# One inference step of a streaming encoder layer: attention's key blocks in two halves, and two moved steps in the projections

## The chip, the cores and the metric

The kernel runs on one core of one Trainium2 chip. The time is the device time of one execution in microseconds (us). The core's engines run programs of their own and meet through semaphores: TensorE (PE, with its weight loads shown as PEld), VectorE (DVE), ScalarE (ACT), GpSimd (POOL) and SyncE (SP, which issues most of the transfers).

## The reference, cut to what matters

One layer is applied to a prompt of 1024 tokens and to a sample of 8 x 16 tokens. What matters here is stick-breaking attention and the expert layer (PEER) behind it:

```
def sb_attend(q, k, v, q_pos, k_pos):
    z = einsum('bqhd,bkhd->bhqk', q, k) / sqrt(HEAD_DIM)
    mask = k_pos[None, :] < q_pos[:, None]
    log_rest = where(mask, log_sigmoid(-z), 0.0)
    suffix = cumsum(log_rest, axis=3, reverse=True) - log_rest
    a = where(mask, exp(log_sigmoid(z) + suffix), 0.0)
    return einsum('bhqk,bkhd->bqhd', a, v)

# the layer, for the prompt and for the sample
xn = rmsnorm(x);  qa, ka, va, qb, kb, vb, ga, gb = split(xn @ w_in)
x = x + (sigmoid(ga) * (sb_attend(qa, ka, va) @ w_oa) + sigmoid(gb) * (sliding(qb, kb, vb) @ w_ob)) @ w_o
x = x + peer(rmsnorm(x))   # 8 heads x top 16 of 128*128 experts: sum of gelu(u[e] . x) * g * v[e]
return rmsnorm(x)
```

## The kernel before, in words

The kernel is five functions in a row, each with a program for every engine: the sample's part (`sample`, `route_sample`, span time 0 to about 335 us), the prompt's projections (`project`, to 764), the sliding window (`window`, to 865), the routing stage (`decide`, to 1735) and the dense expert layer (`dense`, to the end at 3537.6). The diff touches two of them.

**`project`** multiplies the prompt with `w_in`, in 17 blocks of 256 columns (`NBLK`). A weight block is loaded by SP (`refill`, 1 MB), ScalarE rounds it into a high part (`cast`, L1106), VectorE subtracts that from the weights to have the low part (`split`, L994), and TensorE makes three products of high and low parts (L1144). Buffers for parts are three deep (`WB`); TensorE waits for `w_split`, the count of the low parts made, ahead of each block. ScalarE also moves every sum from PSUM (L1101); it casts block b + 3 when it has done so for block b. SP loads block b + 2 when low part b is made.

Beside that work, VectorE and GpSimd do the sample's experts. GpSimd fetches rows of `peer_uv` by number, one for each token at a time, into a ring of 8 buffers, and VectorE's `fetch` takes them in turn: fetches 0 to 127 are multiplied with the tokens and summed (L1074) into the hidden values `h_sb`, ScalarE applies Gelu to all of them at once (L1131, behind weight block `GELU_BLOCK`), and from fetch 128 on VectorE adds the weighted rows (L1079). `weigh` (L1056 to L1060) makes the experts' weights. The order of `split` and `fetch` on VectorE is written out by hand, 15 (`BETWEEN`) fetches to a split.

**`decide`** goes over 8 query tiles t of 128 tokens, and for each over the key blocks n = 0 to t: 36 pairs. A pair's scores for 8 heads are 128 keys x 1024 (heads x queries), in two PSUM banks of 512 columns each. By engine:

- TensorE: `scores` (L2112) writes them, two blocks ahead of use.
- ScalarE's `front` makes log(1 + exp(-|z|)) in three steps (Abs L1985, Exp L1987, Ln L1989).
- VectorE's `logs` adds max(z, 0) (L1755); first it adds the block before to the running sum (`past_logs`, L1747; L1744 at n = 0).
- TensorE's `rests` adds the sums within the block to the scores (`negtri`, L2138, one matmul for each bank; the trace counts each as two) and those of the blocks before (`negone`, L2142).
- ScalarE's `back` (Exp, L1997) makes the weights, and TensorE's `values` (L2152) multiplies them with v.

Between these steps each engine has work of the expert layer's routing of earlier tiles, placed by tables (`WOVEN`, `MADE`): VectorE's searches for the best scores (MAX8 and the like), one-hot rows on VectorE and ScalarE, their products on TensorE (L2102). A tile ends with the output projections and the router's queries (L2195), whose weights come through a ring `c_chunk` that SP loads.

Of the kernel before, what the change touches and what calls it, by code (L numbers as in the profile page):

```python
# [10 lines left out]
ALU = mybir.AluOpType  # L11
ACT = mybir.ActivationFunctionType
# [10 lines left out]
NBLK = IN_COLS // BW  # L23
# [839 lines left out]
def project(nc, a, o, spent, soft, acc, xg, sc, gw, row_v, w_m, x_parts, w_first):  # L863
# [7 lines left out]
    RB = 8  # L871
    ROWS = 84
    LOW = -3e38
    BETWEEN, GELU_BLOCK, WB = 15, 9, 3
    TAKEN = 2 * P - REST
    before = lambda b: PER_T * b if isinstance(b, int) and b <= MIXED else PER_T * MIXED + NG + NP + NP * (b - MIXED - 1)
    flat = lambda x: x.rearrange("p c q -> p (c q)")
    with ExitStack() as ctx:
# [38 lines left out]
        with nc.Block() as block:  # L917
# [70 lines left out]
            def _(dve):  # L988
                nc.vector.memset(top_f[:], 0.0).then_inc(dve_r.sem, 1)

                def split(b):

                    dve.wait_ge(w_high_done, b)
                    nc.vector.tensor_tensor(w_low[b % WB], wbuf[:, b % 2], w_high[b % WB].bitcast(F32), ALU.subtract).then_inc(w_split, 1)  # L994
# [68 lines left out]
                def fetch(first, last):  # L1063

                    for k in range(first, min(last, TAKEN)):
                        r, s = k % RB, k % P
                        if k == P:
                            dve.wait_ge(act_e.sem, act_e.at(0, "gelu"))
                            dve.wait_ge(dve_g.sem, dve_g.at(0, "g"))
                            nc.vector.tensor_tensor(aw[:], h_sb[:], gw[:], ALU.mult).then_inc(dve_g.sem, 1)  # L1070
                            dve.wait_ge(dve_g.sem, dve_g.at(0, "a"))
                        dve.wait_ge(filled[r], 16 * (k // RB + 1))
                        if k < P:
                            nc.vector.scalar_tensor_tensor(ring[:, r], ring[:, r], 1.0, xg[:], ALU.mult, ALU.mult,  # L1074
                                                           accum_out=h_sb[:, s:s + 1]).then_inc(freed, 1)
                        else:
                            if s:
                                dve.wait_ge(summed, s)
                            nc.vector.scalar_tensor_tensor(acc[:], ring[:, r], aw[:, s:s + 1], acc[:], ALU.mult, ALU.add).then_inc(summed, 1)  # L1079
                            dve.wait_ge(summed, s + 1)  # L1080
                            dve.sem_inc(freed, 1)
# [6 lines left out]
                pairs_best()  # L1088
                split(3)
                experts_of()  # L1090
                fetch(0, BETWEEN)
                weigh()
                for b in range(4, NBLK):
                    split(b)
                    fetch(BETWEEN * (b - 3), BETWEEN * (b - 2))

            @block.scalar
            def _(act):
# [284 lines left out]
def decide(nc, a, o, software, acc, aw, row_v, ring, w_o, dense_in, search, ps):  # L1383
# [27 lines left out]
    with ExitStack() as ctx:  # L1411
        sb = lambda n, s, d=F32: ctx.enter_context(nc.sbuf_tensor(n, s, d))
        sem = lambda n: ctx.enter_context(nc.semaphore(n))
# [10 lines left out]
        soft = [sb("c_soft", [P, D])[:], ring[:, 6], ring[:, 7]]  # L1424
# [31 lines left out]
        wide = lambda b: ps[:, b:b + 2, :].rearrange("p b n -> p (b n)")  # L1456
        Z, SUM, TURN = (2, 0, 6), 4, 5
# [10 lines left out]
        G_st, scattered = [sem(f"c_G_st{n}") for n in range(2)], [software[f"c_scattered{q}"] for q in range(FIRST_HOT)]  # L1468
        dve_past = sem("c_dve_past")
        scored, logged, valued = sem("c_scored"), sem("c_logged"), sem("c_valued")  # L1470
        act_f, weighted = Steps(sem("c_act_front"), "abs exp ln", 0), sem("c_weighted")
        softened, past_done = sem("c_softened"), sem("c_past_done")
        pe_m, pe_r = Steps(sem("c_pe_merge"), "mT wo", -1), Steps(sem("c_pe_router"), "xT sc0 sc1 sc2 sc3", -1)
        act_m, act_r = Steps(sem("c_act_merge"), "oaT mT sq ln rms", -1), Steps(sem("c_act_router"), "xT q0 q1 q2 q3 sc0 sc1 sc2 sc3", -1)
# [9 lines left out]
        with nc.Block() as block:  # L1484
# [216 lines left out]
            def _(dve):  # L1701
# [47 lines left out]
                def logs(t, n):  # L1749

                    p = pair(t, n)
                    if n:
                        past_logs(t, n - 1)
                    dve.wait_ge(act_f.sem, act_f.at(p, "ln"))
                    nc.vector.scalar_tensor_tensor(soft[p % 3], wide(Z[n % 3]), 0.0, soft[p % 3], ALU.max, ALU.add).then_inc(softened, 1)  # L1755

                def best16(j, n, src, vals, idx, names, beside=lambda: None):

# [181 lines left out]
            def _(act):  # L1940
# [38 lines left out]
                def front(t, n):  # L1979

                    p = pair(t, n)
                    act.wait_ge(scored, p + 1)
                    if p >= 3:
                        act.wait_ge(valued, p - 2)
                    nc.scalar.activation(soft[p % 3], wide(Z[n % 3]), ACT.Abs).then_inc(act_f.sem, 1)  # L1985
                    act.wait_ge(act_f.sem, act_f.at(p, "abs"))
                    nc.scalar.activation(soft[p % 3], soft[p % 3], ACT.Exp, scale=-1.0).then_inc(act_f.sem, 1)  # L1987
                    act.wait_ge(act_f.sem, act_f.at(p, "exp"))
                    nc.scalar.activation(soft[p % 3], soft[p % 3], ACT.Ln, bias=1.0).then_inc(act_f.sem, 1)  # L1989

                def back(t, n):

# [94 lines left out]
            def _(pe):  # L2087
# [45 lines left out]
                def rests(t, n):  # L2133

                    p, z = pair(t, n), Z[n % 3]
                    pe.wait_ge(softened, p + 1)
                    for par in range(2):
                        last = nc.tensor.matmul(ps[:, z + par, :], negtri[:], soft[p % 3][:, 512 * par:512 * par + 512], start=False, stop=(n == 0), skip_group_check=True)  # L2138
                    if n:
                        pe.wait_ge(past_done, carried(t, n - 1))  # L2140
                        for par in range(2):
                            last = nc.tensor.matmul(ps[:, z + par, :], negone[:], past[:, 512 * par:512 * par + 512], start=False, stop=True, skip_group_check=True)  # L2142
                    last.then_inc(logged, 1)
# [680 lines left out]
```

## Time and profile before

| what | value |
|---|---|
| median of 3 runs (lowest, highest) | 3539.45 us (3533.47, 3540.75) |
| the profiled execution: its time, its span | 3539.31 us, 3537.6 us |
| TensorE busy, share of the span | 3300.8 us, 93% |
| VectorE busy | 2640.3 us, 75% |
| ScalarE busy | 800.3 us, 23% |
| GpSimd busy | 1494.4 us, 42% |

The time is the span and 1.7 us that lie around it. A busy share is an average over all five stages; which engine waits for which is read stage by stage. PEclk and "granted clock" are TensorE's clock as a share of full speed.

### The profile page before, as it was taken

How to read it: one execution, taken by the hardware profiler on the slowest of the kernel's cores; microseconds unless marked ns; L12 is line 12 of the kernel's file. 1: busy time of each engine (PE TensorE's matmuls, PEld its weight loads, DVE VectorE, ACT ScalarE, POOL GpSimd, SP SyncE). 2: the span in 40 equal slices, each digit the busy share in tenths (PEclk: the TensorE clock that was granted, in tenths of full speed). 3: DMA queues.
4: the chain of work that ended last, by engine and by line, in shares of the span. 5: the costliest groups of instructions: out<-in, count | busy, mean ns of one | idle time of the engine just before them, and what ended most of it. 6: DMA issues, size and time to landing. Idle time of an engine off the chain costs nothing.

```text
span 3537.6 us, 43678 instructions
## 1 busy us (share of the span) xinstructions
PE 3300.8 (93%) x14507; PEld 1960.5 (55%) x14516; DVE 2640.3 (75%) x5015; ACT 800.3 (23%) x1589; POOL 1494.4 (42%) x1116
## 2 busy tenths in 40 slices
PE   9769999986888899999899999999999999999997
PEld 7436789984465667677544444444444444444443
DVE  2555888845468767775699998888888777888888
ACT  3542112215122337675100001000010000100001
POOL 0000388710223778886234443444443433434342
PEclk9989999988999999999899999999999999999998
DMA  8988699956887679889899999999999999999997
GB/s 351 414 340 302 225 406 401 403 180 214 335 303 262 176 193 200 209 165 202 324 416 395 416 382 417 411 404 405 417 389 415 375 391 401 383 406 399 397 416 285
DMA packets 465464, 1196.04 MB, mean 338 GB/s; under 512 B 195672, under 2 KB 257800, under 8 KB 386568
## 3 DMA queue, kind: packets, MB, share of 16 engines
q0 software_dynamic: 149776, 679.68, 50.2%
q1 hardware_dynamic: 183472, 495.29, 37.0%
q10 hardware_dynamic: 132048, 19.01, 3.6%
q8 instruction: 85, 1.39, 0.2%
q14 instruction: 83, 0.68, 0.1%
HBM read 1124.51 MB, written 70.39 MB: 338 GB/s over the span
## 4 chain that ended last, share of the span: by engine, by line
PE 33%; DVE 11%; DMA 3%; issue 3%; POOL 0%; DVEq 0%; ACT 0%; POOLq 0%
PE k_ps L2689 17%; PE k_ps L2675 16%; DVE k_yacc L2439 5%; DVE d_ring L2425 4%; DMA d_ring<-peer_uv,d_idx 3%; DVE k_acc L2439 0%; DMA out_y<-k_acc 0%; DVE d_a L2447 0%; DVE d_qacc L2457 0%; POOL d_ring L2387 0%; DVE e_topi L2477 0%; DVE d_aw L2434 0%; DVE e_top L2472 0%; DVE e_sc L2474 0%; DVE e_ci L2477 0%
## 5 line engine op out<-in xcount | busy, mean ns | idle before, releaser
L2387 POOL DMA_INDIRECT d_ring<-peer_uv,d_idx x512 | 691.1, 1350 | 1004.8 <-DVEq L2441 900.3
L2675 PE MATMUL k_ps<-k_xd,k_ring 128*128 128x512 f32 x2016 | 889.4, 594 | 7.8 <-DMA k_ring<-u_blocks 5.2
L2675 PEld LDWEIGHTS k_ps<-k_xd,k_ring 128*128 128x128 f32 x2016 | 384.2, 191 | 493.1 <-issue 486.3
L2425 DVE SCALAR_TENSOR_TENSOR d_ring<-d_ring,k_xn 128x1024 f32<-128x1024 f32 x512 | 607.5, 1221 | 53.8 <-DMA d_ring<-peer_uv,d_idx 31.4
L1687 POOL DMA_INDIRECT G<-c_cellg,c_cell x256 | 434.3, 1696 | 114.7 <-issue 88.7
L2689 PE MATMUL k_ps<-k_ring,d_a 128*128 128x512 f32 x1024 | 453.0, 595 | 10.8 <-DVE d_a L2447 10.0
L2689 PE MATMUL k_ps<-d_v,d_a 128*128 128x512 f32 x1024 | 451.6, 594 | 2.4 <-DVE d_qacc L2457 2.2
L2439 DVE SCALAR_TENSOR_TENSOR k_acc<-d_ring,d_aw,k_acc 128x1024 f32<-128x1024 f32 x256 | 328.9, 1285 | 45.8 <-DVE k_acc L2439 29.7
L2439 DVE SCALAR_TENSOR_TENSOR k_yacc<-d_ring,d_aw,k_yacc 128x1024 f32<-128x1024 f32 x256 | 328.9, 1285 | 37.0 <-DVE k_yacc L2439 25.4
L2689 PEld LDWEIGHTS k_ps<-k_ring,d_a 128*128 128x128 f32 x1024 | 195.1, 191 | 259.1 <-issue 257.0
L2634 ACT ACTIVATE d_a<-k_ps 128x512 f32<-128x512 f32 x128 | 76.3, 597 | 1140.5 <-PE k_ps L2675 1108.9
L2689 PEld LDWEIGHTS k_ps<-d_v,d_a 128*128 128x128 f32 x1024 | 194.8, 191 | 249.6 <-issue 245.5
L2195 PE MATMUL k_ps<-c_mT,c_chunk 128*128 128x128 f32 x2048 | 248.1, 281 | 18.9 <-DMA c_chunk<-wq 17.8
L2195 PEld LDWEIGHTS k_ps<-c_mT,c_chunk 128*128 128x128 f32 x2048 | 242.4, 198 | 24.7 <-DMA c_chunk<-wq 19.3
L984 POOL DMA_INDIRECT k_merge<-peer_uv,a_rowu x128 | 165.3, 1291 | 180.3 <-DVE k_rowv L1052 140.7
L1074 DVE SCALAR_TENSOR_TENSOR k_merge<-k_merge,k_xg 128x1024 f32<-128x1024 f32 x128 | 153.6, 1225 | 43.6 <-DMA k_merge<-peer_uv,a_rowu 32.6
L1144 PE MATMUL a_ps<-a_w_high,k_x_part 128*128 128x256 f32 x896 | 169.1, 289 | 5.5 <-issue 4.9
L1653 POOL DMA_INDIRECT k_ring<-peer_uv,k_rowv x56 | 66.7, 1190 | 213.8 <-DVE k_acc L1857 95.7
L2630 ACT ACTIVATE d_ge<-d_h (+1 forms) x256 | 49.0, 200 | 475.4 <-DVE d_ring L2425 475.3
L1144 PEld LDWEIGHTS a_ps<-a_w_high,k_x_part 128*128 128x128 f32 x896 | 144.4, 197 | 8.1 <-issue 7.6
L2447 DVE TENSOR_TENSOR d_a<-d_a,d_gb 128x512 f32<-128x512 f32 x128 | 88.2, 690 | 69.1 <-issue 35.6
L1144 PE MATMUL a_ps<-a_w_low,k_x_part 128*128 128x256 f32 x448 | 129.7, 290 | 2.4 <-issue 2.2
(423 smaller groups left out, 4265.5 us busy)
## 6 DMA issues: line engine op xcount, KB each, us to landing
c_chunk<-wq SPq DMA_DIRECT2D x128, 512.0 KB
k_ring<-u_blocks SPq DMA_DIRECT2D x128, 512.0 KB, 21.1
s_kc<-sb_kT SPq DMA_DIRECT2D x32, 1024.0 KB, 13.7
s_vc<-sb_v SPq DMA_DIRECT2D x32, 1024.0 KB, 11.2
c_chunk<-w_m SPq DMA_DIRECT2D x64, 512.0 KB
k_ring<-v_blocks SPq DMA_DIRECT2D x64, 512.0 KB, 9.5
d_gb<-G SPq DMA_DIRECT2D x32, 1024.0 KB
d_v<-v_blocks SPq DMA_DIRECT2D x64, 512.0 KB
```

The costliest lines, as they stand in the source:

```text
L984: pool.indirect_dma_start(out=ring[:, k % RB], out_offset=None, in_=rows, in_offset=bass.IndirectOffsetOnAxis(ap=source[:, k % P:k % P + 1 ...
L1074: nc.vector.scalar_tensor_tensor(ring[:, r], ring[:, r], 1.0, xg[:], ALU.mult, ALU.mult, accum_out=h_sb[:, s:s + 1]).then_inc(freed, 1)
L1144: last = nc.tensor.matmul(out, lhsT(left, k), rhs(right, k), start=(k == 0 and n == 0), stop=(k == KC - 1 and n == 2))
L1687: pool.indirect_dma_start(out=grid, out_offset=bass.IndirectOffsetOnAxis(ap=cell[q][:, s:s + 1], axis=0), in_=cell_g[q][:, s:s + 1], in_of ...
L2195: last = nc.tensor.matmul(ps[:, QUERY[w // 4], (w % 4) * P:(w % 4 + 1) * P], wq[:, c * P:(c + 1) * P], xT[:, c], start=(c == 0), stop=(c = ...
L2387: pool.indirect_dma_start(out=ring[:, b], out_offset=None, in_=a["peer_uv"], in_offset=bass.IndirectOffsetOnAxis(ap=idx8[par][:, b:b + 1], ...
L2425: last = nc.vector.scalar_tensor_tensor(ring[:, b, 0:D], ring[:, b, 0:D], 1.0, xn[T % 2][:], ALU.mult, ALU.mult, accum_out=h[:, bass.ds(co ...
L2439: nc.vector.scalar_tensor_tensor(acc[T % 2][:], ring[:, b, D:], aw[:, bass.ds(col + n, 1)], acc[T % 2][:], ALU.mult, ALU.add).then_inc(sum ...
L2447: nc.vector.tensor_tensor(A[u][j][:], A[u][j][:], gb[u][:, j], ALU.mult).then_inc(gated, 1)
L2634: nc.scalar.activation(A[x // GB][x % GB][:], ps[:, HB + x % 2, :], ACT.Gelu).then_inc(h_gelu, 1)
L2675: last = nc.tensor.matmul(ps[:, HB + x % 2, :], ub[j][:, k], xd[:, k].rearrange("p t q -> p (t q)"), start=(k == 0), stop=(k == KC - 1))
L2689: last = nc.tensor.matmul(ps[:, to, :], A[u][j][:, q * P:(q + 1) * P], vb[u][j][:, half * 512:half * 512 + 512], start=(opens and j == 0), ...
```

## The change

In `project`, `GELU_BLOCK` goes from 9 to 10, so ScalarE's program has the Gelu one weight block later; and each `split` from 4 on stands one step of 15 fetches earlier in VectorE's program. In `decide`, `front`, `logs` and `rests` treat the two banks of a pair one after the other: ScalarE makes Abs, Exp and Ln for the first 512 columns and then for the others, VectorE adds max(z, 0) to each half when its Ln is there, and TensorE waits for each half ahead of its `negtri` products. `past_logs`, `negone`, `back` and `values` stay whole.

```diff
-    BETWEEN, GELU_BLOCK, WB = 15, 9, 3
+    BETWEEN, GELU_BLOCK, WB = 15, 10, 3
...
                 experts_of()
+                split(4)
                 fetch(0, BETWEEN)
                 weigh()
-                for b in range(4, NBLK):
-                    split(b)
-                    fetch(BETWEEN * (b - 3), BETWEEN * (b - 2))
+                for b in range(5, NBLK + 1):
+                    if b < NBLK:
+                        split(b)
+                    fetch(BETWEEN * (b - 4), BETWEEN * (b - 3))
...
-                    dve.wait_ge(act_f.sem, act_f.at(p, "ln"))
-                    nc.vector.scalar_tensor_tensor(soft[p % 3], wide(Z[n % 3]), 0.0, soft[p % 3], ALU.max, ALU.add).then_inc(softened, 1)
+                    for par in range(2):
+                        half = soft[p % 3][:, 512 * par:512 * par + 512]
+                        dve.wait_ge(act_f.sem, act_f.at(p, f"ln{par}"))
+                        nc.vector.scalar_tensor_tensor(half, ps[:, Z[n % 3] + par, :], 0.0, half, ALU.max, ALU.add).then_inc(softened, 1)
...
-                    nc.scalar.activation(soft[p % 3], wide(Z[n % 3]), ACT.Abs).then_inc(act_f.sem, 1)
-                    act.wait_ge(act_f.sem, act_f.at(p, "abs"))
-                    nc.scalar.activation(soft[p % 3], soft[p % 3], ACT.Exp, scale=-1.0).then_inc(act_f.sem, 1)
-                    act.wait_ge(act_f.sem, act_f.at(p, "exp"))
-                    nc.scalar.activation(soft[p % 3], soft[p % 3], ACT.Ln, bias=1.0).then_inc(act_f.sem, 1)
+                    for par in range(2):
+                        half = soft[p % 3][:, 512 * par:512 * par + 512]
+                        nc.scalar.activation(half, ps[:, Z[n % 3] + par, :], ACT.Abs).then_inc(act_f.sem, 1)
+                        act.wait_ge(act_f.sem, act_f.at(p, f"abs{par}"))
+                        nc.scalar.activation(half, half, ACT.Exp, scale=-1.0).then_inc(act_f.sem, 1)
+                        act.wait_ge(act_f.sem, act_f.at(p, f"exp{par}"))
+                        nc.scalar.activation(half, half, ACT.Ln, bias=1.0).then_inc(act_f.sem, 1)
...
-                    pe.wait_ge(softened, p + 1)
                     for par in range(2):
+                        pe.wait_ge(softened, 2 * p + par + 1)
                         last = nc.tensor.matmul(ps[:, z + par, :], negtri[:], soft[p % 3][:, 512 * par:512 * par + 512], start=False, stop=(n == 0), skip_group_check=True)
```

VectorE's program in `project` around the first fetches, before and then in the difference (L1050 and L1052 make the row numbers for the fetches, L1074 is a fetched row's product, L994 a low part):

```order
206 L1049 TENSOR_SCALAR a_h<-a_cand 128x128
207 L1050 CAST a_rowu<-a_h 128x128
208 L1052 TENSOR_SCALAR k_rowv<-a_rowu 128x128
209 L1074 SCALAR_TENSOR_TENSOR k_merge,a_h<-k_merge,k_xg 128x1024 x15
210 L1056 TENSOR_REDUCE a_gsum<-k_aw 128x8
211 L1058 RECIPROCAL a_gsum<-a_gsum 128x8
212 L1060 TENSOR_TENSOR k_aw<-k_aw,a_gsum 128x128
213 L994 TENSOR_TENSOR a_w_low<-k_merge,a_w_high 128x2048
```

```order
 L1050 CAST a_rowu<-a_h 128x128
 L1052 TENSOR_SCALAR k_rowv<-a_rowu 128x128
+L994 TENSOR_TENSOR a_w_low<-k_merge,a_w_high 128x2048
 L1074 SCALAR_TENSOR_TENSOR k_merge,a_h<-k_merge,k_xg 128x1024 x15
 L1056 TENSOR_REDUCE a_gsum<-k_aw 128x8
 L1058 RECIPROCAL a_gsum<-a_gsum 128x8
 L1060 TENSOR_TENSOR k_aw<-k_aw,a_gsum 128x128
-L994 TENSOR_TENSOR a_w_low<-k_merge,a_w_high 128x2048
-L1074 SCALAR_TENSOR_TENSOR k_merge,a_h<-k_merge,k_xg 128x1024 x15
 L994 TENSOR_TENSOR a_w_low<-k_merge,a_w_high 128x2048
```

Low part 4 now stands ahead of the first 15 fetches, and all later ones follow one group of fetches sooner.

ScalarE's program in `project` around the Gelu (L1131; L1133 in the changed kernel), before and then after (L1101 and L1103 are evacuations of sums, L1106 and L1108 casts, ACT_TABLE_LOAD loads a function table):

```order
253 L1101 ACT_TABLE_LOAD
254 L1101 ACTIVATE a_stage<-a_ps 128x256 x8
255 L1106 ACTIVATE k_w_first<-k_merge 128x2048
256 L1131 ACT_TABLE_LOAD
257 L1131 ACTIVATE a_h<-a_h 128x128
258 L1101 ACT_TABLE_LOAD
259 L1101 ACTIVATE a_stage<-a_ps 128x256 x8
```

```order
254 L1103 ACTIVATE a_stage<-a_ps 128x256 x8
255 L1108 ACTIVATE k_w_first<-k_merge 128x2048
256 L1103 ACTIVATE a_stage<-a_ps 128x256 x8
257 L1108 ACTIVATE a_w_high<-k_merge 128x2048
258 L1133 ACT_TABLE_LOAD
259 L1133 ACTIVATE a_h<-a_h 128x128
260 L1103 ACT_TABLE_LOAD
261 L1103 ACTIVATE a_stage<-a_ps 128x256 x8
```

Eight evacuations and a cast now stand ahead of the Gelu and its table loads.

ScalarE's program in `decide`, before (one pair's `back`, then the `front` of the next but one) and after (one `front`; L1991, L1993 and L1995 are its lines there):

```order
521 L1997 ACTIVATE c_soft<-k_ps 128x1024
522 L1951 ACTIVATE c_spread<-k_ps 128x4x128
523 L1985 ACTIVATE k_ring<-k_ps 128x1024
524 L1987 ACTIVATE k_ring<-k_ring 128x1024
525 L1989 ACTIVATE k_ring<-k_ring 128x1024
```

```order
567 L1991 ACTIVATE c_soft<-k_ps 128x512
568 L1993 ACTIVATE c_soft<-c_soft 128x512
569 L1995 ACTIVATE c_soft<-c_soft 128x512
570 L1991 ACTIVATE c_soft<-k_ps 128x512
571 L1993 ACTIVATE c_soft<-c_soft 128x512
572 L1995 ACTIVATE c_soft<-c_soft 128x512
```

Three instructions of 1024 columns became six of 512; on VectorE the one instruction of L1755 became two in the same place.

## Rows read from the trace of the kernel before

**Rows 1.** The page's first part: busy us of each engine (share of the span).

```profile
PE 3300.8 (93%) x14507; PEld 1960.5 (55%) x14516; DVE 2640.3 (75%) x5015; ACT 800.3 (23%) x1589; POOL 1494.4 (42%) x1116
```

**Rows 2.** Windows: length, busy us (count) of PE, PEld, DVE, ACT, POOL, clock, DMA share, GB/s.

```profile
480.00:640.00 160.00, 152.29 (x1144) 146.56 (x1145) 131.39 (x188) 32.43 (x58) 129.16 (x99) 0.94 1.02 403
...
865.00:1735.00 870.00, 784.44 (x4901) 561.96 (x4910) 582.87 (x1880) 370.15 (x596) 500.92 (x312) 0.96 0.83 236
```

**Rows 3.** TensorE's timeline, starts of blocks 4 and 6 [idle before, what ended it].

```profile
431.93 0.80 PE L1144 MATMUL a_ps<-k_x_part,a_w_high 128*128 128x512 f32 x1 [2.16 <-DVE a_w_low L994]
...
479.84 2.93 PE L1144 MATMUL a_ps<-k_x_part,k_w_first 128*128 128x512 f32 x6 [2.57 <-issue]
```

**Rows 4.** VectorE's timeline in `project`: the first fetch, low parts 4 and 6.

```profile
403.66 1.23 DVE L1074 SCALAR_TENSOR_TENSOR k_merge<-k_merge,k_xg 128x1024 f32<-128x1024 f32 x1 [4.66 <-DMA k_merge<-peer_uv,a_rowu]
...
429.59 2.29 DVE L994 TENSOR_TENSOR a_w_low<-k_merge,a_w_high 128x2048 fp32r<-128x2048 f32 x1
...
477.50 2.29 DVE L994 TENSOR_TENSOR k_w_first<-k_merge,k_w_first 128x2048 fp32r<-128x2048 f32 x1
```

**Rows 5.** Windows behind the two waits, and one behind the first's slow stretch.

```profile
431.80:435.20 3.40, 3.27 (x8) 2.59 (x9) 3.40 (x6) 0.90 (x2) 2.58 (x2) 0.50 1.05 414
435.30:438.70 3.40, 3.40 (x16) 2.80 (x16) 3.40 (x8) 0.00 (x0) 3.10 (x2) 1.00 1.01 374
...
479.70:483.00 3.30, 3.16 (x8) 2.49 (x9) 3.30 (x6) 0.60 (x1) 2.88 (x2) 0.50 1.04 423
```

**Rows 6.** ScalarE's timeline in `project`: cast 4, the Gelu, the last evacuation.

```profile
384.36 1.91 ACT L1106 ACTIVATE a_w_high<-k_merge 128x2048 fp32r<-128x2048 f32 x1
...
614.70 0.31 ACT L1131 ACTIVATE a_h<-a_h 128x128 f32<-128x128 f32 x1 [9.50 <-issue]
...
763.37 0.38 ACT L1101 ACTIVATE a_stage<-a_ps 128x256 f32<-128x256 f32 x1 [2.49 <-PE a_ps L1144]
```

**Rows 7.** VectorE's timeline: its last fetched row in `project`.

```profile
734.10 1.28 DVE L1079 SCALAR_TENSOR_TENSOR k_acc<-k_merge,k_aw,k_acc 128x1024 f32<-128x1024 f32 x1 [0.21 <-DVE k_acc L1079]
```

**Rows 8.** One line's view, L1755: idle before it (us, times), and who waited for it.

```profile
  ACT k_ring L1989: 23.2, 8
...
  PE k_ps L2138: 45.4, 24
```

**Rows 9.** Groups by line and shape: instructions of 512 columns (the sample stage's).

```profile
L332 DVE TENSOR_TENSOR s_work<-s_ps,s_work 128x512 f32<-128x512 f32 x32 | 22.1, 691 | 1.1
...
L452 ACT ACTIVATE s_work<-s_work 128x512 f32<-128x512 f32 x32 | 20.2, 631 | 0.0
...
L449 ACT ACTIVATE s_work<-s_ps 128x512 f32<-128x512 f32 x32 | 19.1, 596 | 67.0 <-PE s_ps L611 67.0
```

**Rows 10.** Timelines of three engines in `decide`, pair (4, 1).

```profile
1201.67 1.02 ACT L1985 ACTIVATE k_ring<-k_ps 128x1024 f32<-128x1024 f32 x1 [11.63 <-PE k_ps L2112]
...
1203.81 1.06 ACT L1989 ACTIVATE k_ring<-k_ring 128x1024 f32<-128x1024 f32 x1
...
1204.90 1.23 DVE L1755 SCALAR_TENSOR_TENSOR k_ring<-k_ps,k_ring 128x1024 f32<-128x1024 f32 x1 [0.45 <-ACT k_ring L1989]
...
1206.18 1.98 PE L2138 MATMUL k_ps<-k_ring,c_negtri 128*128 128x512 f32 x4 [1.55 <-DVE k_ring L1755]
```

**Rows 11.** Timelines of VectorE and TensorE in `decide`, tile 7, two pairs in a row.

```profile
1576.62 1.21 DVE L1755 SCALAR_TENSOR_TENSOR k_ring<-k_ps,k_ring 128x1024 f32<-128x1024 f32 x1
...
1581.97 1.20 DVE L1747 TENSOR_TENSOR c_past<-c_past,k_ring 128x1024 f32<-128x1024 f32 x1
1583.24 1.22 DVE L1755 SCALAR_TENSOR_TENSOR c_soft<-k_ps,c_soft 128x1024 f32<-128x1024 f32 x1
...
1577.89 1.99 PE L2138 MATMUL k_ps<-k_ring,c_negtri 128*128 128x512 f32 x4 [0.85 <-DVE k_ring L1755]
```

**Rows 12.** One line's view, L2195: TensorE's idle before the router's queries (us, times).

```profile
  DMA c_chunk<-wq: 37.1, 16
```

**Rows 13.** One line's view, L1997: ScalarE's idle before `back` (us, times).

```profile
  DVE c_past L1747: 30.3, 18
```

More of the change, by code:

```diff
@@ L1470, in decide @@
         scored, logged, valued = sem("c_scored"), sem("c_logged"), sem("c_valued")
-        act_f, weighted = Steps(sem("c_act_front"), "abs exp ln", 0), sem("c_weighted")
+        act_f, weighted = Steps(sem("c_act_front"), "abs0 exp0 ln0 abs1 exp1 ln1", 0), sem("c_weighted")
         softened, past_done = sem("c_softened"), sem("c_past_done")
```

## The prediction

> **What bounds the kernel now.** I read the page's totals first: TensorE is busy 93% of the span, VectorE 75%, ScalarE 23% [rows 1]. A kernel like this loses time only where TensorE stands still or runs slowly, so I took the windows of the two stages that the diff touches, then TensorE's timeline at each of its waits there, and then the lines that it waited for. In the projections TensorE has nearly no idle time except at two places: ahead of weight block 4 it sat idle for 2.16 us until VectorE's low part was made, and ahead of block 6 for 2.57 us [rows 3]. The second carries the label "issue", which names no engine, but VectorE's low part 6 runs from 477.50 to 479.79 and TensorE resumes at 479.84 [rows 3, 4]: that is the same wait. Block 5's low part came in time in between. Behind both waits stands a stretch at a granted clock of 0.50, the lower of the clock's two levels (1.2 instead of 2.4 GHz): 8 matmuls in 3.40 us where 16 fit at 1.00 [rows 5].
>
> In the routing stage TensorE is busy 784.44 of 870 us [rows 2], so 86 us are idle. Of these, 45.4 us in 24 pieces are waits of the `negtri` products for VectorE's L1755, the very step that is cut in two [rows 8]; 37.1 us in 16 pieces are waits for the router's weights from DMA [rows 12]. The first number looks like the prize. The question is whether shortening one link of that chain shortens the chain.
>
> **Projections: what the change takes away.** Low part 4 now stands ahead of the first 15 fetches. There VectorE sits idle 4.66 us until the first fetched row lands at 403.66 [rows 4], and the cast it needs was done at 384.36 + 1.91 = 386.27 [rows 6]. The low part takes 2.29 us [rows 4], so it runs from about 399.0 to 401.3 inside idle time, 28 us ahead of TensorE's need (431.93 - 2.16 = 429.77). Each later low part takes the place of the one before it. Blocks 4 and 5 together take 479.84 - 431.93 = 47.9 us, so a block is some 24 us; part 5 is made at about 429.6 to 431.9 and is needed at about 452, part 6 near 453.5 to 455.8 and needed near 472. Both waits go:
>
> - idle time: 2.16 + 2.57 = 4.73 us [rows 3];
> - the slow stretches: a matmul at full clock takes 3.40 / 16 = 0.2125 us; 8 fewer were done in the first, about 7.5 fewer in the second [rows 5]; 15.5 x 0.2125 = 3.3 us.
>
> Together 8.0 us. TensorE's last sum of the stage is moved out at 763.37, with VectorE done at 734.10 + 1.28 = 735.4 [rows 6, 7], so the stage's end follows TensorE and the 8.0 us reach the end of the kernel: the later stages start when this one ends.
>
> **What could take it back there.** A low part made sooner also releases SP's load of the block after next sooner. It is 1 MB, 2.6 us at the 403 GB/s of [rows 2], and falls among the first fetched rows; they may come 2.6 us later on VectorE, whose slack at the stage's end is 28 us, 20 once TensorE ends 8 sooner. The casts may now be what some low parts wait for, on VectorE, with `fetch` queued behind; I bound this by a few us, against the same slack, since TensorE needs the part a block later.
>
> **The later Gelu.** Gelu waited 9.50 us on ScalarE for VectorE's fetches and ran at 614.70 [rows 6]; eight evacuations were queued behind it, but TensorE's eight banks covered them, and it shows no gap there: no gain on TensorE. Afterwards ScalarE comes to it one block (24 us) later: 24 - 9.5 = 14.5 us, less up to 8 because TensorE is sooner. VectorE has then 6 to 15 us of waiting ahead of fetch 128, and GpSimd's ring stands still behind it. With 735.4 + 15 = 750 against TensorE's new end at about 755, this costs nothing; if the cover were gone, every us past 755 would count in full.
>
> **Attention in halves, on ScalarE.** One pair's front takes 3.20 us now (1201.67 to 1203.81 + 1.06) [rows 10]. No row shows it in halves of this stage; the nearest are the sample's 512-column steps, 0.596 out of PSUM and 0.631 in SBUF [rows 9]. So a half takes 0.60 + 2 x 0.63 and 0.06 between: 1.92 us; both take 3.84 us if nothing overlaps. The first half is ready 1.28 us sooner, the second 0.64 us later than before.
>
> **On VectorE and TensorE.** L1755 takes 1.23 us, and 0.05 later TensorE starts [rows 10]. A 512-column step with two sources takes 0.691 [rows 9]; two take 1.38, at most 0.16 more than one whole.
>
> Two kinds of pairs follow. Where VectorE waits for ScalarE, as in (4, 1) with 0.45 us [rows 10], the second half's product could start at 3.20 + 0.03 + 1.23 + 0.05 + 0.91 = 5.42 after the front's start (0.91 being the first product's share of the 1.98); it will start at 3.84 + 0.03 + 0.69 + 0.05 = 4.61. Gain 0.8 us, inside the 1.55 us of idle time ahead of it. Where VectorE itself is the pace, as in tile 7 (1583.24 follows 1581.97 + 1.20 with no wait, 6.6 us after the last L1755 [rows 11]), TensorE may start after 0.69 instead of 1.22: gain 0.53 us of its 0.85.
>
> But VectorE gets no faster. Its next L1755 stands behind the same searches and running sums, and those have no wait for TensorE to lose. TensorE therefore arrives early and waits longer at the next pair: the gain is had about once a tile, at the last pair, not 24 times. Against it stand up to 0.16 us more VectorE work in each pair. Tiles 4 to 7 have 26 pairs: four gains of 0.53 to 0.8 are 2.1 to 3.2 us, 26 x 0.16 are up to 4.2. The net lies between -3.2 and +2.1; I take 0. Tiles 0 to 3 end in waits for the router's weights from DMA [rows 12], which swallow a us either way. TensorE's 36 added waits are met while the first half's product runs; by the 0.05 us of the row they cost 1.8 at most, and I take nothing.
>
> **Sum.** The profiled execution took 3539.31 us, 0.14 below the median of the runs shown. 3539.31 - 8.0 + 0 = 3531.3, so 3531.
>
> **Rivals.**
>
> *The gains add up.* If TensorE, not VectorE, were the pace of the tiles, each of the 24 waits would lose 0.53: 12.7 us of the 45.4 [rows 8]. For it: the idle time is real and ends at L1755. Against: VectorE runs from one L1755 to the next without a wait in tile 7 [rows 11]. Time 3531.3 - 12.7 = 3518.6.
>
> *Other stalls eat the projections' gain.* From 480 to 640 TensorE loses 160 - 152.29 = 7.7 us idle, at a mean clock of 0.94 (another 9.6), while DMA is at its full share of 1.02 [rows 2]; there "issue" again names no engine. The moved loads and fetches re-phase that stretch. One more such stall, of 2.6 (as [rows 3]) to 8.7 (half of that loss), gives 3534 to 3540. For it: the stretch has such losses already. Against: they may as well shrink.
>
> *Slower: ScalarE becomes the pace.* Its front is 0.64 us longer in each pair. If that lay in the path of tiles 4 to 7, 26 x 0.64 = 16.6 us: 3548. It decides where ScalarE's idle time ahead of `back` is under 0.64 us; now that is 30.3 / 18 = 1.7 us on average, waiting for VectorE's sum [rows 13], and ScalarE is busy only 370 of the stage's 870 us [rows 2]. So this is unlikely, but single pairs will meet it.
>
> The Trainium skill, "VectorE: DVE Perf Modes", section on the TRN2 errata, speaks against the change here: each instruction on VectorE and ScalarE with a source in SBUF pays a fixed latency, so a large tile pays it once and many small ones each time. This trace agrees: 1.06 us for 1024 columns [rows 10] against 0.631 for 512 [rows 9]. By that rule alone, with all of it on the path, the time would be this rival's 3548; by the rows on who waits for whom it is the 3531 of the sum.
>
> *The Gelu comes too late.* If VectorE ended past 755, the stage would end later: 3534 to 3540 for 3 to 9 us past it.
>
> **Chances and range.** Forecast (projections' 8 us, attention about nothing; own range 3526 to 3536) 0.55; gains add up 0.15; other stalls 0.20; ScalarE the pace 0.07; Gelu 0.03. This kernel's measurement tells about 0.2%, 7.1 us, from no change: faster is below 3532.4, slower above 3546.5. Some 0.65 of the forecast's range lies below 3532.4: faster 0.55 x 0.65 + 0.15 = 0.51; same 0.55 x 0.35 + 0.20 + 0.03 = 0.42; slower 0.07. The range goes from the first rival to the second's end, 3519 to 3540, and leaves out the slower rival and the tails, about 0.17.
>
> **What will show it.** Right: no idle time ahead of TensorE's blocks 4 and 6 and no half clock behind them; the last evacuation near 755; VectorE idle ahead of its first L1079 without harm; the sum of TensorE's waits for VectorE's L1755 smaller by much, but moved to the other waits, with the routing stage still about 870 us long. Wrong: a routing stage shorter than 864 us (gains add up) or longer than 876 (ScalarE's idle time ahead of `back` gone, TensorE's `values` waiting for it); or new "issue" gaps between 400 and 640 us.

## The result, and the profile after

The changed kernel takes 3514.8 us (median of 4 runs, 3506.39 to 3518.24), against 3539.74 for the kernel before: a ratio of 0.9929, 95% interval 0.9911 to 0.9947, which is 25 us. Forecast were 3531, with a range of 3519 to 3540. The direction held; the time lies under the range, with three times the gain that the sum had.

The first part of the page, of after, beside [rows 1] (busy us, share of the span):

```profile
PE 3292.3 (94%) x14507; PEld 1953.6 (56%) x14516; DVE 2645.1 (75%) x5051; ACT 819.7 (23%) x1697; POOL 1487.5 (42%) x1116
```

VectorE has 36 and ScalarE 108 instructions more; hardly any busy time has gone. The stages come first, therefore. Each stage's length, from its first instruction to the next stage's first, in the profiled executions:

```
stage          before   after   difference
sample          340.0   342.6     +2.6
projections     428.5   406.8    -21.7
window           94.6   100.0     +5.4
routing         876.5   877.5     +1.0
dense layer    1798.0  1787.0    -11.0
```

The routing stage, where attention was cut in halves, is no shorter. The dense layer, in which no line was changed, is 11 us shorter. The projections give nearly three times the 8.0 us of the sum, in this pair of profiles. (The sample's and the window's differences belong to untouched code; over the runs below these stages lie between 338 and 344, and 94.6 and 100.4, with and without the edits.)

The projections after. VectorE's timeline (low part 4, the last fetched row), ScalarE's (the Gelu, the last evacuation) and TensorE's only idle piece over 0.3 us behind its first matmul there:

```profile
401.58 2.28 DVE L994 TENSOR_TENSOR a_w_low<-k_merge,a_w_high 128x2048 fp32r<-128x2048 f32 x1
...
740.82 1.28 DVE L1079 SCALAR_TENSOR_TENSOR k_acc<-k_merge,k_aw,k_acc 128x1024 f32<-128x1024 f32 x1 [0.26 <-DMA k_merge<-peer_uv,k_rowv]
```

```profile
621.58 0.31 ACT L1133 ACTIVATE a_h<-a_h 128x128 f32<-128x128 f32 x1 [20.02 <-DVE k_merge L1074]
...
739.18 0.38 ACT L1103 ACTIVATE a_stage<-a_ps 128x256 f32<-128x256 f32 x1 [2.49 <-PE a_ps L1146]
```

```profile
623.73 2.50 PE L1146 MATMUL a_ps<-k_w_first,k_x_part 128*128 128x256 f32 x19 [2.67 <-ACT a_stage L1103]
```

Low part 4 runs where it was forecast, and the waits of [rows 3] are gone. But ScalarE now stands 20.02 us at the Gelu for VectorE's fetches (9.50 in [rows 6]), and TensorE has a new wait of 2.67 us, for a sum's bank that ScalarE has not moved out. TensorE's last sum is moved out at 739.56 and VectorE is done at 742.10, but neither ends the stage. SP issues its last two stores of `gates` at 739.59 and 740.81, and the next stage starts at 749.45, when they have landed. SP's wait for them, before and then after:

```profile
SPq L972 <- DMA gates<-a_stage: 3.1, 1, 3.1
```

```profile
SPq L972 <- DMA gates<-a_stage: 7.4, 1, 7.4
```

The line's view of SP's last two loads (`k_merge<-bd`, 1 MB each, issued 15 us ahead of the stores) has 18.4 and 21.4 us from issue to landing, 7.1 and 9.4 before. TensorE's work in the stage, from its first matmul to the end of its last, got 27 us shorter (396.4 for 423.3), the stage only 22.

Windows (columns as in [rows 2]) of the same stretch as there, and of the routing stage and the dense layer by their own bounds, after:

```profile
480.00:640.00 160.00, 157.33 (x1308) 156.41 (x1307) 134.25 (x193) 34.26 (x64) 122.92 (x98) 1.00 1.02 409
...
849.70:1727.20 877.50, 795.87 (x4910) 564.13 (x4918) 586.85 (x1922) 388.67 (x709) 500.84 (x312) 0.95 0.83 235
1727.20:3513.90 1786.70, 1748.89 (x4064) 772.29 (x4064) 1508.66 (x2286) 153.33 (x427) 720.81 (x586) 0.99 0.98 398
```

and the same two stages of before:

```profile
863.10:1739.60 876.50, 788.55 (x4910) 563.48 (x4918) 583.97 (x1885) 373.01 (x600) 500.92 (x312) 0.96 0.83 235
1739.60:3537.60 1798.00, 1754.95 (x4064) 774.11 (x4064) 1507.61 (x2288) 150.61 (x427) 722.89 (x586) 0.99 0.98 396
```

Attention's chain did get shorter link by link. One line's view of who waited for VectorE's step (L1759), after, and of the matmuls' idle time at `values`, before (L2152) and then after (L2158):

```profile
  PE k_ps L2144: 33.6, 25
```

```profile
  DMA c_v<-out_v: 2.8, 2
```

```profile
  DMA c_v<-out_v: 7.9, 2
```

TensorE waits 33.6 us for VectorE's step instead of 45.4 [rows 8], nearly the 12.7 of the first rival. The stage did not follow: the matmuls' wait for `values`' v blocks rose from 2.8 to 7.9 us, and TensorE's busy time rose by 7.3 at a granted clock of 0.95 instead of 0.96. In all, TensorE's idle time there fell by 6.3 us.

### The profile page after: what moved, and what is told of

It is laid out like the page before. It is cut to its first block, busy times and chain, and to the rows that moved or that the text cites. A ratio compares the mean times of both kernels' runs of the same rounds, so it can differ in the third digit from the quotient of the medians.

```text
span 3513.9 us, 43822 instructions
## 1 busy us (share of the span) xinstructions
PE 3292.3 (94%) x14507; PEld 1953.6 (56%) x14516; DVE 2645.1 (75%) x5051; ACT 819.7 (23%) x1697; POOL 1487.5 (42%) x1116
## 4 chain that ended last, share of the span: by engine, by line
PE 36%; DVE 9%; DMA 3%; issue 2%; POOL 0%; DVEq 0%; ACT 0%; POOLq 0%
PE k_ps L2695 18%; PE k_ps L2681 18%; DVE d_ring L2431 3%; DVE k_yacc L2445 3%; DMA d_ring<-peer_uv,d_idx 3%; DVE k_acc L2445 1%; DMA out_y<-k_yacc 0%; DVE d_a L2453 0%; POOL d_ring L2393 0%; DVE d_qacc L2463 0%; DVE e_topi L2483 0%; DVE e_top L2478 0%; DVE d_aw L2440 0%; DVE e_sc L2480 0%; DVE e_ci L2483 0%
## 5 line engine op out<-in xcount | busy, mean ns | idle before, releaser
L1074 DVE SCALAR_TENSOR_TENSOR k_merge<-k_merge,k_xg 128x1024 f32<-128x1024 f32 x128 | 154.3, 1225 | 44.9 <-DMA k_merge<-peer_uv,a_rowu 43.3
L1146 PE MATMUL a_ps<-a_w_high,k_x_part 128*128 128x256 f32 x896 | 161.4, 283 | 0.0
L2453 DVE TENSOR_TENSOR d_a<-d_a,d_gb 128x512 f32<-128x512 f32 x128 | 88.1, 689 | 64.5 <-ACT d_a L2640 25.6
```

What stands on the lines that cost most here:

```text
L1146: last = nc.tensor.matmul(out, lhsT(left, k), rhs(right, k), start=(k == 0 and n == 0), stop=(k == KC - 1 and n == 2))
L2453: nc.vector.tensor_tensor(A[u][j][:], A[u][j][:], gb[u][:, j], ALU.mult).then_inc(gated, 1)
```

## The experiments

Ratios are to the kernel before, measured on the same chip, with 95% intervals. Stage lengths are those of the one profiled execution of each kernel, by the same bounds as above. Edits are shown cut to the lines that matter.

**One part of the change at a time.** Four kernels.

`e1_proj`: the two edits of `project`, with the old `decide`.

> Only the two edits of the projections; attention whole as before. Theory A (the whole gain comes from the projections stage: the two waits for low parts, 8 us, and the instruction gaps of blocks 3, 7 and 8 that went with them, some 15 us; attention gives nothing): about 3516 to 3520, TensorE's work of the stage some 396 us long as in the changed kernel (423 before). Theory B (attention's halves give about half of the gain): 3526 to 3532.

`e2_halves`: the three edits of `decide`, with the old `project`.

> Only attention in halves; the projections as before. Theory A: 3536 to 3541, no change, the routing stage 876 to 878 us. Theory B: 3524 to 3530, with the 11 us of the dense stage shorter as in the changed kernel. The projections of this kernel are a second look at the old order: if the instruction gaps at blocks 3, 7 and 8 come again, they belong to that order; if they lie elsewhere or are missing, they are scatter from run to run.

`e3_splits`: the kernel before with only the low parts sooner.

```diff
-                fetch(0, BETWEEN)
-                weigh()
-                for b in range(4, NBLK):
-                    split(b)
-                    fetch(BETWEEN * (b - 3), BETWEEN * (b - 2))
+                split(4)
+                fetch(0, BETWEEN)
+                weigh()
+                for b in range(5, NBLK + 1):
+                    if b < NBLK:
+                        split(b)
+                    fetch(BETWEEN * (b - 4), BETWEEN * (b - 3))
```

> Only the low parts sooner, Gelu behind block 9 as before. Theory A: the two waits ahead of blocks 4 and 6 are gone, 8 us; ScalarE stands at the Gelu while sums of block 10 pile up, so TensorE may stand up to 10 us there if the fetches have not gained: 3518 to 3532. Rival (the later Gelu is what brings the other part): over 3528.

`e4_gelu`: the kernel before with only this.

```diff
-    BETWEEN, GELU_BLOCK, WB = 15, 9, 3
+    BETWEEN, GELU_BLOCK, WB = 15, 10, 3
```

> Only the Gelu one block later, low parts in the old order. Theory A: no gain by itself, 3536 to 3542, the waits ahead of blocks 4 and 6 as before. Rival (ScalarE's stall at the Gelu was what held TensorE in the projections): 3525 or less.

```
kernel      ratio   95% interval       projections  routing  dense
e1_proj     0.9957  0.9941 to 0.9973      409.1      879.3   1798.1
e2_halves   0.9967  0.9953 to 0.9981      423.3      878.6   1785.7
e3_splits   1.0011  1.0000 to 1.0023      423.3      875.0   1798.2
e4_gelu     0.9994  0.9981 to 1.0006      420.2      878.4   1798.3
```

Theory A was wrong that the whole gain comes from the projections: the halves have 12 us of it. It was right that attention has none: the 12 us are in the dense layer, which is 1798 us long in every kernel of the table with the old `decide`. And neither edit of the projections is worth anything alone: sooner low parts gain nothing, the later Gelu gains nothing, both together gain 15 us.

The rows say why. TensorE's timeline of `e3_splits`, at its only idle piece over 0.3 us behind its first matmul there, and ScalarE's there:

```profile
615.03 0.55 PE L1146 MATMUL a_ps<-a_w_low,k_x_part 128*128 128x256 f32 x1 [21.80 <-ACT a_stage L1103]
```

```profile
612.88 0.31 ACT L1133 ACTIVATE a_h<-a_h 128x128 f32<-128x128 f32 x1 [39.16 <-DVE k_merge L1074]
```

TensorE got past blocks 4 and 6 without waiting, and then stood 21.80 us: ScalarE's program had the Gelu ahead of the evacuations of block 10, the Gelu waits for VectorE's fetch 127, and eight banks of sums were full. What it had won it lost there. The Gelu is a meeting of three engines: VectorE has done 128 fetched rows at about 613 to 622 us in these kernels' profiles, wherever TensorE is, and TensorE cannot get more than eight sums past the block named by `GELU_BLOCK`. The profile of `e2_halves`, with the old `project`, has the same meeting (8.8 to 12.0 us in its profile and those of `e5_act` to `e8_fill128` below, which have the old `project` too):

```profile
619.51 0.55 PE L1144 MATMUL a_ps<-a_w_low,k_x_part 128*128 128x256 f32 x1 [11.63 <-ACT a_stage L1101]
```

In `e4_gelu` the meeting is a block later, but TensorE does not get there sooner, since the low parts are what it waits for, ahead of blocks 4 and 6 as in [rows 3] and then also later. Two rows of its TensorE timeline:

```profile
654.59 0.39 PE L1144 MATMUL a_ps<-a_w_low,k_x_part 128*128 128x256 f32 x1 [2.25 <-DVE a_w_low L994]
680.12 0.39 PE L1144 MATMUL a_ps<-a_w_low,k_x_part 128*128 128x256 f32 x1 [2.24 <-DVE a_w_low L994]
```

So one edit lets TensorE run ahead and the other gives it room to do so. The instruction gaps that the profile of before has in blocks 3, 7 and 8 do not come again in blocks 7 and 8 of `e2_halves` and `e4_gelu`, which have the old order: there they were scatter, and in the execution shown they stood in place of the wait at the Gelu. So that execution is no fair measure of the old order: its projections took 428.5 us, against 419.5 to 423.8 in the five other profiles with the old `project`, and the stage's 21.7 us of gain are some 15 beside those.

**What shortens the dense layer.** Two kernels with one half of the halves each, and two without any.

`e5_act`: the kernel before with ScalarE's `front` in halves, as in the change; VectorE waits for the second Ln and does its step whole.

```diff
-                    dve.wait_ge(act_f.sem, act_f.at(p, "ln"))
+                    dve.wait_ge(act_f.sem, act_f.at(p, "ln1"))
```

> The kernel before, with only ScalarE's front in halves: VectorE's step and TensorE's wait whole again. Theory P (the halves gain nothing in attention; what they gain is 12 us in the untouched dense stage, because VectorE's program is 36 instructions longer ahead of it and its instruction loads fall elsewhere): VectorE's program is as long as before, so the dense stage is 1798 us and the time that of before, or up to 5 us more by the longer front. Theory Q (ScalarE's part is what shifts the dense stage): dense stage 1786, time 12 us under before.

`e6_dve`: the kernel before with VectorE's step and TensorE's wait in halves, both behind the whole Ln; VectorE's edit:

```diff
-                    dve.wait_ge(act_f.sem, act_f.at(p, "ln"))
-                    nc.vector.scalar_tensor_tensor(soft[p % 3], wide(Z[n % 3]), 0.0, soft[p % 3], ALU.max, ALU.add).then_inc(softened, 1)
+                    for par in range(2):
+                        half = soft[p % 3][:, 512 * par:512 * par + 512]
+                        dve.wait_ge(act_f.sem, act_f.at(p, "ln"))
+                        nc.vector.scalar_tensor_tensor(half, ps[:, Z[n % 3] + par, :], 0.0, half, ALU.max, ALU.add).then_inc(softened, 1)
```

> The kernel before, with only VectorE's step and TensorE's wait in halves; ScalarE's front whole. Theory P: 36 more VectorE instructions, the dense stage 1786 us, the routing stage about 877, the time some 10 us under before. Theory Q: dense stage 1798, time as before.

`e7_fill36`: the kernel before, with waits that are already met at the start of VectorE's program in `decide`.

```diff
-                dve.wait_ge(tabs, 64)
+                for _ in range(37):
+                    dve.wait_ge(tabs, 64)
```

> The kernel before with nothing of the change, but 36 waits on VectorE (for a semaphore that has been reached) at the start of the routing stage, where VectorE is idle: only the length of its program changes. Theory P: dense stage 1786 us, time some 10 us under before. Theory R (the halves move the dense stage by what attention hands over: other times, other transfers): dense stage 1798, time as before.

`e8_fill128`: the same with 129 in place of 37.

> As the kernel with 36 such waits, but 128. The trace's instruction loads of VectorE are of 8 KB each; if only the place within such a piece counts, and one instruction is 64 bytes, then 128 instructions shift by a whole piece and theory P gives the dense stage of before again, 1798 us. If the length acts in another way: any value between 1780 and 1805, and not that of the kernel with 36 waits.

Two such waits make one instruction, as the traces' counts show: VectorE's program was 18 and 64 instructions longer, not 36 and 128.

```
kernel       more on VectorE   ratio   95% interval       routing  dense
e5_act             0           1.0013  1.0002 to 1.0024    883.1   1795.2
e6_dve            36           0.9959  0.9945 to 0.9974    879.5   1785.2
e7_fill36         18           0.9974  0.9962 to 0.9987    882.2   1788.1
e8_fill128        64           1.0001  0.9987 to 1.0014    876.0   1797.8
```

Theory P holds against Q and R: a kernel that has nothing of the change but 18 idle waits is 9 us faster than the kernel before, all of it in the dense layer, and with 64 waits the gain is gone. (The expectation on 128 more instructions, by its reckoning a whole 8 KB piece, was not put to the test.) The dense layer of `e5_act` is 2.8 us shorter than that of before; its cause is open.

The rows show what happens. VectorE's timeline of before has this three times (2757, 2869 and 2987 us), here the last, and TensorE's what came of it. The first two held TensorE for 1.1 and 1.7 us, the last for 7.0:

```profile
2987.31 0.69 DVE L2447 TENSOR_TENSOR d_a<-d_a,d_gb 128x512 f32<-128x512 f32 x1 [10.77 <-issue]
```

```profile
2996.67 2.07 PE L2689 MATMUL k_ps<-k_ring,d_a 128*128 128x512 f32 x2 [7.03 <-DVE d_a L2447]
```

VectorE stood 10.77 us for nothing that the profile names. The DMA view of just that idle time (2976.5 to 2987.3) names it, two packets of the queue that loads instructions:

```profile
q0 software_dynamic: 566, 4.08, 91.8%
q1 hardware_dynamic: 95, 0.39, 8.8%
q14 instruction: 2, 0.02, 0.4%
```

The place is a loop's jump back. In the trace the two loads start 5.0 us apart (2980.27 and 2985.30), and VectorE's idle time falls into two pieces of 5.39 and 4.93 us, the first right behind the branch. The changed kernel has five such jumps with one load each, this one the third, and TensorE's idle time is short:

```profile
2526.99 0.69 DVE L2453 TENSOR_TENSOR d_a<-d_a,d_gb 128x512 f32<-128x512 f32 x1 [5.91 <-issue]
```

```profile
2536.34 7.13 PE L2695 MATMUL k_ps<-k_ring,d_a 128*128 128x512 f32 x16 [1.24 <-DVE d_a L2453]
```

In `e8_fill128` the double load is back, at another turn of a loop (VectorE's timeline, then TensorE's):

```profile
2545.99 0.69 DVE L2448 TENSOR_TENSOR d_a<-d_a,d_gb 128x512 f32<-128x512 f32 x1 [10.64 <-issue]
```

```profile
2555.35 5.48 PE L2690 MATMUL k_ps<-k_ring,d_a 128*128 128x512 f32 x6 [6.92 <-DVE d_a L2448]
```

The 7.03 us of TensorE's idle time are followed by a stretch at a lower clock. Windows of before, behind that wait and a little later:

```profile
2996.70:3003.40 6.70, 6.70 (x10) 2.88 (x11) 6.06 (x10) 0.20 (x1) 3.65 (x3) 0.60 0.94 335
3007.00:3013.70 6.70, 6.70 (x17) 2.96 (x16) 6.14 (x10) 0.34 (x1) 2.27 (x2) 1.00 1.02 425
```

Seven matmuls fewer, of 6.70 / 17 = 0.39 us each, are 2.8 us; the clock of 0.60 for 6.70 us says the same, 2.7. So 7.03 + 2.8 = 9.8 us are lost at this jump, most of the 10 to 13 us by which the dense layer is shorter in the kernels without it. The rest, up to 3 us, stays unexplained.

The Trainium skill, "Runtime: NRT & Kernel Launch", section on instruction fetch mechanics, has this rule: a taken branch whose target lies outside the pages that an engine holds forces a load before execution goes on. The runs agree: VectorE stood 5.91 us at a jump with one load here, and 10.77 where two follow one another.

**Whether attention's halves gain anything, and how far the meeting can be moved.** Four kernels on one chip.

`e9_proj_fill`: the edits of `project`, attention whole, and 73 waits as above (36 more VectorE instructions by the count).

> The two edits of the projections, attention whole as before, and 36 more instructions (waits that are met) on VectorE at the start of the routing stage, as many as the halves add there. Theory P+G (the projections gain by the meeting at the Gelu, the rest is the place of VectorE's program in its instruction loads, attention's halves give nothing): dense stage 1786 us, the time that of the whole change, 0.992 to 0.994 of before. Rival (the halves do gain in attention): about 0.9957, as the projections' edits alone, or up to 5 us under it.

`e10_gelu11`: the changed kernel with one number more.

```diff
-    BETWEEN, GELU_BLOCK, WB = 15, 10, 3
+    BETWEEN, GELU_BLOCK, WB = 15, 11, 3
```

> The changed kernel with the Gelu behind block 11 instead of 10. Theory G (TensorE meets VectorE's fetch 128 at the Gelu): the gap of TensorE near 621 us is gone and its work in the stage 3 to 6 us shorter, but VectorE waits for the Gelu some us and ends the stage at 742 or later, so the time is that of the changed kernel, -4 to +6 us. Rival (the place of the Gelu is what the stage's end follows, as from 9 to 10): 10 us or more under the changed kernel.

`e11_again`: the changed kernel, unchanged.

> The changed kernel itself once more, beside the others on one chip: 0.991 to 0.995 of before in every theory; its profile shows whether TensorE's gap at the Gelu and the dense stage of 1787 us come again.

`e12_proj_dve`: the edits of `project` with `e6_dve`'s attention.

> The changed kernel with ScalarE's front whole again: projections' edits, VectorE's step and TensorE's wait in halves. By the runs so far ScalarE's halves alone cost about 5 us: 0 to 8 us under the changed kernel, the routing stage 876 to 880 us. Rival (ScalarE's halves are what lets the halves on VectorE gain): slower than the changed kernel by 3 us or more.

```
kernel         ratio   95% interval       median   projections  routing  dense
e9_proj_fill   0.9928  0.9914 to 0.9943   3508.1      406.6      872.7   1787.8
e10_gelu11     0.9923  0.9910 to 0.9937   3507.2      407.1      878.7   1786.0
e11_again      0.9942  0.9928 to 0.9955   3513.7      406.4      872.1   1788.1
e12_proj_dve   0.9931  0.9916 to 0.9946   3506.8      408.1      872.6   1786.0
```

With attention whole and 36 instructions of waits in the place of the halves, `e9_proj_fill` has all of the gain. In the profiles of these runs the routing stage is 872.1 to 878.7 us long with the whole change in `decide` and 872.7 to 882.2 with attention whole: no difference to be seen. (`e12_proj_dve`, with 872.6, lies under the 876 to 880 that were expected of it.)

Behind block 11 the meeting costs TensorE nothing more, but VectorE waits for the Gelu, as expected, and ends at 744.93. The stage is as long all the same, and again it is the last stores that end it. VectorE's timeline of `e10_gelu11` at the Gelu, and SP's wait for the stores there:

```profile
625.05 0.29 DVE L1070 TENSOR_TENSOR k_aw<-a_h,k_aw 128x128 f32<-128x128 f32 x1 [3.70 <-ACT a_h L1133]
```

```profile
SPq L972 <- DMA gates<-a_stage: 8.1, 1, 8.1
```

In all six profiles with both edits of `project` the last store landed 2.4 to 2.5 us behind the second of SP's last loads, and the next stage started 0.8 us later, whether VectorE ended at 740.6 (`e11_again`) or at 744.9. That the loads and rows still on their way are what holds the stores back is read from these times; no run moved them.

`e9_proj_fill`, `e10_gelu11` and `e12_proj_dve` have medians 6 to 7 us under the changed kernel's (`e11_again`), but their intervals overlap with its own; whether one of them is faster is open. For `e10_gelu11`, -4 to +6 us had been expected.

## Why the prediction was wrong, point by point

Two terms of the sum failed, both put at nothing. The later Gelu ("no gain on TensorE") decides whether the low parts' 8.0 us arrive at all: without it they gave nothing, with it the projections gave 15.2. And the dense layer, in which no line changes, gave 11.7. That the kernel would be faster was right, in part by luck, for nearly half of the gain lies where none was forecast; and the first rival's 3518.6 lies nearest to the measured time by luck alone, since the waits that it counts on gave nothing.

- **The two waits for low parts: right, but not their worth.** Both went, and so did the slow stretches behind them. The step that failed is "the stage's end follows TensorE and the 8.0 us reach the end of the kernel". They do not by themselves: `e3_splits` gains nothing, because TensorE meets the Gelu. With the Gelu a block later the kernel gets 15 us faster (`e1_proj`: 0.0043 x 3535.5 = 15.2), more than 8.0, since the later meeting also takes away most of what TensorE waited there with the old order: 11.63 us in the profile of `e2_halves`, 2.3 to 5.8 in the five with both edits and the Gelu behind block 10.
- **The later Gelu: wrong.** The text had the eight evacuations that queued behind it, said that TensorE's eight banks covered them, and put its gain at nothing. They covered them only because gaps earlier in that one execution had held TensorE back; in the five other profiles with the old `project` TensorE waits there. The row that told it was there: 9.50 us of ScalarE's idle time at the Gelu [rows 6], with "issue" as its label. The next question was who comes late if TensorE gets 8 us ahead, and it was not asked of this row.
- **VectorE's waiting for the Gelu: wrong.** 6 to 15 us were worked out; it was 0.38 us in the profile, for ScalarE was there 20 us too early, not too late. The bound added a block's 24 us, less up to 8, to ScalarE's arrival of before, 614.70 - 9.50 = 605.2; with TensorE so far ahead it came at 621.58 - 20.02 = 601.6.
- **The stage's end: wrong.** It was to follow TensorE, with 20 us of slack for VectorE. TensorE got 24 us ahead of its old end and VectorE 7 behind its own, and the end now follows neither, but the landing of the last stores, for which SP waits 7.4 us instead of 3.1.
- **Attention: right.** The gain of single links is real (33.6 us of waits instead of 45.4) and does not add up: +1.0 us in the routing stage, against bounds of -3.2 to +2.1. (The text's 870 us are the window 865 to 1735; by its own bounds the stage was 876.5 before.) The prices taken from the sample's stage held: halves took 0.585 and 0.630 us on ScalarE and 0.69 on VectorE. One reading was wrong: the 37.1 us of [rows 12] add the waits of the weight loads to those of the matmuls; the matmuls alone waited 17.8 us, in 8 pieces. The slower rival did not come: its condition was idle time under 0.64 us ahead of `back`, and what VectorE's sum left there was 25.6 us in 15 pieces, 1.7 each, even in `e5_act`, where VectorE stays whole. That kernel is 0.0013 slower, with a routing stage 6.6 us longer than that of before in its profile; but with attention whole the stage's length alone lies between 872.7 and 882.2.
- **Left out altogether: the place of the code.** The sum held no term for the dense layer, since no line of it changes. 36 more VectorE instructions in front of it are worth 0.0033 x 3535.5 = 11.7 us (`e2_halves`, whose routing stage is no shorter), and 18 waits alone (`e7_fill36`) 0.0026 x 3534.3 = 9.2. The halves' 11.7 and the projections' 15.2 are 26.9, where 25 were measured.

Open is what the six kernels with both edits would gain if the last stores landed as before. Open is also why TensorE had its instruction gaps in blocks 7 and 8 of the execution shown; it was not tried. Open too is which lengths of VectorE's program give one load and which two: of those run, 18 and 36 more give one, 0 and 64 two.

## What to carry to other kernels

Where one engine's program holds a step that waits for another engine's last item, everything behind it in that program waits too; gains made by a third engine ahead of such a meeting are worth nothing until the meeting moves, so look for the longest idle time in front of a single instruction before you add up the waits. When a stage's engines all end sooner, look at the transfers that still have to land: they may end it now. A kernel whose stages are written as loops can get 10 us faster or slower by the mere length of the program in front of them: before a gain is put down to an edit, see in which stage it lies, and run the kernel before with as many idle instructions. A wait that shrinks in its own row is a gain only if the stage is shorter.

## What the runs showed of the hardware

- At a loop's jump back VectorE stood idle for 0.4 to 2.8 us where it waited for no instruction load, 5.4 to 6.4 us where it waited for one and 10.1 to 10.9 us for two in a row (the dense layers of all profiles; DMA share 0.98 in before and after); the profile labels it "issue", and only the DMA view shows the load.
- A store of 512 KB at the end of the projections landed 2.6 and 3.6 us after its issue when the stage's rows and loads had landed (`e2_halves`), and 5.7 and 7.9 us after it when loads of 1 MB, issued before it, were still on their way (the changed kernel).
- Two waits in a row on VectorE for a semaphore that was reached became one instruction; each such instruction took 0.05 us.
- Runs of one kernel scatter by up to 20 us (before: 3527 to 3548 in 30 runs), while the dense layer's length is the same within 0.3 us in the profiles of before, `e1_proj`, `e3_splits` and `e4_gelu`: the length of a stage that scatters little can tell in one profile what the time of a run can't. The routing stage is none of these: 877.5 and 872.1 us in two profiles of the changed kernel.
